# A hybrid encoder layer with product-key experts: both ends reordered, and the routing's table of sums cut from 256 to 144 places

## What is computed

```
h = x + W_out[concat(short gated conv, SSD scan)](RMSNorm(x))
h = h + CrossAttn(RMSNorm(h), 256 memory tokens)
h = h + PEER(RMSNorm(h));   y = RMSNorm(h) * final_norm_w

def block(xb):                                   # PEER, 8 heads, top 16, 128 x 128 experts
    q = (xb @ w_pq).reshape(-1, PEER_HEADS, 2, PEER_DK_HALF)
    sc = einsum('thpd,hpkd->thpk', q, sub_keys)
    v1, i1 = top_k(sc[:, :, 0], 16);  v2, i2 = top_k(sc[:, :, 1], 16)
    comb = (v1[..., :, None] + v2[..., None, :])             # 16 x 16 sums of a head
    cidx = (i1[..., :, None] * N_KEYS + i2[..., None, :])
    top_sc, pos = top_k(comb, 16);  eidx = take_along_axis(cidx, pos)
    gate = softmax(top_sc);  hid = gelu(einsum('td,thkd->thk', xb, u_tab[eidx]))
    return einsum('thk,thkd->td', gate * hid, v_tab[eidx])
```

## Time and profile before

| what | value |
|---|---|
| runs shown (3) | median 1840.97 us, 1833.16 to 1843.06 |
| the profiled execution | 1838.45 us, with a span of 1836.7 us from the first to the last instruction |
| mean granted TensorE clock | 0.963 |
| TensorE matmul (PE) busy | 1689.9 us, 92% |
| DVE busy | 1225.0 us, 67% |
| GpSimd (POOL) busy | 697.7 us, 38% |
| ACT busy | 369.2 us, 20% |
| HBM read and written | 539.46 MB and 21.66 MB |

### The profile page before, as it was taken

One profiled execution on the slowest core, in us unless ns is written; L12 is line 12 of the kernel. 1 busy time (PEld: TensorE's weight loads), 2 busy tenths in 40 slices (PEclk: granted clock), 3 DMA queues, 4 the chain that ended last, 5 costly groups with the idle time before them and its releaser, 6 DMA issues. The chain is left out here.

```text
span 1836.7 us, 19834 instructions
## 1 busy us (share of the span) xinstructions
PE 1689.9 (92%) x7088; PEld 1256.1 (68%) x7088; DVE 1225.0 (67%) x2437; ACT 369.2 (20%) x912; POOL 697.7 (38%) x598
## 2 busy tenths in 40 slices
PE   6998999999777888898896999999999999999996
PEld 5887888877655677787785666666666666666542
DVE  1252111799688768898986999676656666656675
ACT  1031123111330244642660001101000000000101
POOL 0000000234124437731664555555444544534551
PEclk9999999999878999899898999999999999999998
DMA  5532444779336949995999999999999999999995
GB/s 168 180 110 99 153 138 138 240 249 349 101 134 204 379 167 367 338 329 184 361 346 415 409 409 410 409 407 410 406 409 410 397 410 409 396 409 405 377 409 221
DMA packets 238301, 563.10 MB, mean 307 GB/s; under 512 B 17068, under 2 KB 125276, under 8 KB 236156
## 3 DMA queue, kind: packets, MB, share of 16 engines
q0 software_dynamic: 82944, 302.03, 42.7%
q1 hardware_dynamic: 121512, 242.72, 36.1%
q10 hardware_dynamic: 33748, 17.10, 3.1%
HBM read 539.46 MB, written 21.66 MB: 306 GB/s over the span
## 5 line engine op out<-in xcount | busy, mean ns | idle before, releaser
L782 POOL DMA_INDIRECT M<-in_u_tab,IDX x288 | 331.3, 1150 | 736.5 <-DVE PEER L1742 358.0
L789 POOL DMA_INDIRECT M<-in_v_tab,IDX x288 | 362.8, 1260 | 369.2 <-DVE X L1763 299.3
L1093 PE MATMUL PSB<-XN,M 128*128 128x256 f32 x2048 | 469.0, 384 | 12.2 <-ACT M L1303 6.0
L1101 PE MATMUL PSB<-M,HST 128*128 128x512 f32 x1024 | 461.3, 596 | 10.4 <-DVE HST L1819 9.6
L1093 PEld LDWEIGHTS PSB<-XN,M 128*128 128x128 f32 x2048 | 393.5, 193 | 112.8 <-issue 53.2
L1742 DVE CUSTOM_DVE_ANT_0 M<-M,XN 128x1024 f32<-128x1024 f32 x288 | 351.8, 1223 | 146.7 <-DMA M<-in_u_tab,IDX 135.3
L1763 DVE SCALAR_TENSOR_TENSOR X<-M,PEER,X 128x1024 f32<-128x1024 f32 x256 | 328.1, 1282 | 101.4 <-DMA M<-in_v_tab,IDX 88.0
L831 PE MATMUL PSB<-M 128*128 128x256 f32 (+1 forms) x1408 | 333.4, 398 | 10.2 <-DVE M L1399 8.9
L1101 PEld LDWEIGHTS PSB<-M,HST 128*128 128x128 f32 x1024 | 194.8, 191 | 215.1 <-issue 198.5
L831 PEld LDWEIGHTS PSB<-M 128*128 128x128 f32 x1408 | 270.1, 193 | 66.4 <-DVE M L1399 9.8
L838 PE MATMUL PSB<-M 128*128 128x256 f32 (+1 forms) x1056 | 247.7, 395 | 2.5 <-DVE M L1399 1.6
(11 more groups left out here) (214 smaller groups left out, 1072.7 us busy)
## 6 DMA issues: line engine op xcount, KB each, us to landing
M<-in_u_blocks SPq DMA_DIRECT2D x128, 512.0 KB
M<-in_v_tab SPq DMA_DIRECT2D x128, 512.0 KB
M<-in_w_in SPq DMA_DIRECT2D x24, 1024.0 KB
M<-in_w_pq SPq DMA_DIRECT2D x16, 1024.0 KB
gate_spill<-M ACTq DMA_DIRECT2D x16, 1024.0 KB, 14.5
M<-gate_spill SPq DMA_DIRECT2D x16, 1024.0 KB, 11.1
M<-in_w_out SPq DMA_DIRECT2D x8, 1024.0 KB
M<-in_w_mq SPq DMA_DIRECT2D x8, 1024.0 KB
```

The source lines that it names most:

```text
L782: pool.indirect_dma_start(out=UA[:, s % RR, :], out_offset=None, in_=utab, in_offset=bass.IndirectOffsetOnAxis(ap=IDX[:, n:n + 1], axis=0) ...
L789: pool.indirect_dma_start(out=VA[:, s % RR, :], out_offset=None, in_=vtab, in_offset=bass.IndirectOffsetOnAxis(ap=IDX[:, n:n + 1], axis=0) ...
L1093: last = pe.matmul(PSB[:, 4 + b % 2, 0:2 * P], UBLK[:, b % SR, c, :], XN[:, 1:3, c * P:(c + 1) * P], start=(c == 0), stop=(c == DC - 1))
L1101: last = pe.matmul(PSB[:, 2 * t + hf, :], WR[:, b % WRING, t * P:(t + 1) * P], VBLK[:, b % SR, hf * 512:(hf + 1) * 512], start=(b == 0), s ...
```

## The change

1. Start. Tile 1's rows are loaded right after tile 0's. Five of the nine small loads and that of `state_ssd` are issued by SP, between and behind the first big loads. The sum of squares of tile 1 is taken by DVE (`sq`), not ACT, and `const` stands behind tile 0's `norm`.
2. End. `fold` stands ahead of the last `vd`. The first half of that `vd` has a semaphore of its own, for which the first `close` waits. The order of leaving is tile 4, 1, 2, with all three `leave` steps ahead of all three `final` steps.
3. Routing. The table of sums has 8 x 16 sums and 16 more places (8 of them filled with a very small number, 8 with the sums of rows 8 to 15 and column 0). Three instructions of the decoding are added: a `min`, a mask, and for tiles 1 and 2 a copy.
4. The planner's estimate for a piece of `rt` is 1.75 us instead of 1.9.

```diff
@@ dense
-        s += [("const",)]
-        for t in TG[0]:
-            s += [("norm", 0, t), ("turn", 0, t)]
+        s += [("sq", 1), ("norm", 0, 0), ("const",), ("norm", 0, 1), ("turn", 0, 0), ("turn", 0, 1)]
@@ DVE_US
-          "a1": 3.8, "norm": 1.2, "keep": 0.3, "rt": 1.9, "smd": 0.8, ...
+          "a1": 3.8, "norm": 1.2, "keep": 0.3, "rt": 1.75, "smd": 0.8, ...
@@ plan
+        if b == NBLK - 1:
+            out.append(("fold",))
         out.append(("vd", b))
...
-    for t in DENSE:
-        out += [("close", t), ("leave", t), ("final", t)]
-    return out + [("fold",), ("leave", NP), ("final", NP)]
+    out += [("close", t) for t in DENSE] + [("leave", t) for t in CLOSED]
+    return out + [("final", t) for t in CLOSED]
@@ SP
             sp.dma_start(X[:, 0, :], xp[0]).then_inc(x_in[0], 16)
+            sp.dma_start(X[:, 1, :], xp[1]).then_inc(x_in[1], 16)
+            for row in SMALL_ROWS[4:]:
+                load_small(sp, *row)
             load_block(sp, 0)
-            sp.dma_start(X[:, 1, :], xp[1]).then_inc(x_in[1], 16)
             load_block(sp, 1)
+            sp.dma_start(S0[:, :, :], a["state_ssd"]...).then_inc(state_in, 16)
             load_block(sp, 2)
@@ TensorE, vd
+                    if b == NBLK - 1 and t == 0:
+                        last.then_inc(first_closed, 1)
@@ ACT, norm
+                if (ph, t) == (0, 1):
+                    act.wait_ge(sq_done, 1)
+                    col = ROOTS.index(("norm", 0, 1))
+                    act.activation(SS[:, col:col + 1], SS[:, col:col + 1], ACT.Sqrt, bias=EPSC[:, :], scale=1.0 / D).then_inc(root_done, 1)
+                    return
@@ DVE
+            def sq(t):
+                col = ROOTS.index(("norm", 0, t))
+                dve.wait_ge(const_ok, 1)
+                dve.wait_ge(x_in[t], 16)
+                dve.tensor_tensor_reduce(XN[:, t, :], X[:, t, :], X[:, t, :], 1.0, 0.0, ALU.mult, ALU.add, SS[:, col:col + 1]).then_inc(sq_done, 1)
@@ DVE, keys2
-                    also(dve.tensor_tensor(CO, bc(TV[:, 0, :].unsqueeze(2), [P, TOPK, TOPK]), bc(TV[:, 1:2, :], [P, TOPK, TOPK]), ALU.add))
+                    also(dve.tensor_tensor(COF[:, 0:8 * TOPK].rearrange("p (a b) -> p a b", a=8), bc(TV0[:, 0:8].unsqueeze(2), [P, 8, TOPK]),
+                                           bc(TV1.unsqueeze(1), [P, 8, TOPK]), ALU.add))
+                    also(dve.tensor_scalar(COF[:, 8 * TOPK:NCO], TV0[:, 8:24], TV1[:, 0:1], None, ALU.add))
@@ DVE, experts
-                    also(dve.tensor_scalar(CA[:, 0:2, :], CP, 4, 7, ALU.logical_shift_right, ALU.logical_shift_left))
-                    also(dve.tensor_scalar(CA[:, 2:4, :], CP, 15, 7, ALU.bitwise_and, ALU.logical_shift_left))
+                    also(dve.tensor_scalar(CPA[:, 1], CP, 8 * TOPK, None, ALU.min))
...
+                    sync()
+                    also(dve.tensor_scalar(CA, CPA.rearrange("p a z k -> p (a z) k"), 7, None, ALU.logical_shift_left))
...
+                    also(dve.tensor_reduce(EQS, places, AXX, ALU.min))
+                    sync()
+                    also(dve.tensor_scalar(EQS, EQS, NK - 1, None, ALU.bitwise_and))
...
-                        dve.sem_inc(topk_done, 1)
+                        dve.tensor_copy(I12[:, t - 1, :, 2 * TOPK * pair:2 * TOPK * (pair + 1)], EQS).then_inc(topk_done, 1)
@@ DVE, close
-                dve.wait_ge(vd_done, NBLK)
+                if t == DENSE[0]:
+                    dve.wait_ge(first_closed, 1)
+                else:
+                    dve.wait_ge(vd_done, NBLK)
```

More of the change, by code:

```diff
@@ L22 @@
 PH, NK, TOPK = 8, 128, 16
+NCO = 9 * TOPK
 EPS = 1e-6
@@ L145 @@
 DVE_US = {"turn": 1.4, "memn": 2.4, "in": 0.3, "ca": 2.1, "cs": 2.2, "dt": 3.5, "s1": 2.6, "s2": 2.4, "s3": 4.8, "s4": 1.4, "o": 0.45, "mo": 0.45,
-          "a1": 3.8, "norm": 1.2, "keep": 0.3, "rt": 1.9, "smd": 0.8, "tt": 0.6, "oh": 1.25, "d": 1.3, "v": 1.3, "final": 1.3}
+          "a1": 3.8, "norm": 1.2, "keep": 0.3, "rt": 1.75, "smd": 0.8, "tt": 0.6, "oh": 1.25, "d": 1.3, "v": 1.3, "final": 1.3}
 EARLY_STEPS = 5
@@ L517, in build_program @@
         TS2 = take_(2, P)
[L518 to L522, removed]
+        TV0, TV1, TI = take_(3 * 8), take_(TOPK), take_(2, 2, TOPK, u=True)
+        TOPS = [[TV0[:, 0:8], TV0[:, 16:24]], [TV1[:, 0:8], TV1[:, 8:16]]]
+        COF = take_(NCO)
+        CO2 = take_(NCO)
+        CPA = take_(2, 2, TOPK, u=True)
+        take_(1024 - 2 * NCO - 4 * TOPK)
         EQF = cut(PT_, g_[0] - 1024, 1024).bitcast(U32)
-        CP = take_(2, TOPK, u=True)
+        CP = CPA[:, 0]
         CA, KEY = [cut(PT_, 4 * TOPK * k, 4, TOPK).bitcast(U32) for k in range(2)]
-        TAGF = take_(TOPK)
+        TAGF = take_(2, TOPK)
         TAG = TAGF.bitcast(U32)
-        EQS = cut(PT_, 8 * TOPK, 2, 2 * TOPK)
+        EQS = cut(PT_, 8 * TOPK, 2, 2 * TOPK).bitcast(U32)
         SCS = take_(2, 256)
@@ L1658, in keys @@
                     for h in range(2):
-                        also(dve.max(TV[:, h, 0:8], src[:, h, :]))
+                        also(dve.max(TOPS[h][0], src[:, h, :]))
                     sync()
                     for h in range(2):
-                        also(dve.max_index(TI[:, h, z, 0:8], TV[:, h, 0:8], src[:, h, :]))
-                        also(dve.match_replace(TS2[:, h, :], TV[:, h, 0:8], src[:, h, :], NEG))
+                        also(dve.max_index(TI[:, h, z, 0:8], TOPS[h][0], src[:, h, :]))
+                        also(dve.match_replace(TS2[:, h, :], TOPS[h][0], src[:, h, :], NEG))
                 def keys2(z):
@@ L1700, in experts @@
                     places = EQF.rearrange("p (a j k) -> p a j k", a=2, k=TOPK)
-                    if t in DENSE:
-                        also(dve.tensor_reduce(I12[:, t - 1, :, 2 * TOPK * pair:2 * TOPK * (pair + 1)], places, AXX, ALU.min))
-                    else:
-                        also(dve.tensor_reduce(EQS, places, AXX, ALU.min))
+                    also(dve.tensor_reduce(EQS, places, AXX, ALU.min))
+                    sync()
+                    also(dve.tensor_scalar(EQS, EQS, NK - 1, None, ALU.bitwise_and))
                     if (t, pair) == (NP, 0) or pair == PH // 2 - 1:
@@ L1833, in final @@
                 dve.scalar_tensor_tensor(out=x, in0=x, scalar=rs, in1=GAIN[0:n, :], op0=ALU.mult, op1=ALU.mult).then_inc(y_norm, 1)
-            does = {"const": const, "state": state, "norm": norm, "turn": turn, "memn": memn, "in": in_, "keep": keep, "ca": ca, "cs": cs, "dt": dt, "oc": oc,
+            does = {"sq": sq, "const": const, "state": state, "norm": norm, "turn": turn, "memn": memn, "in": in_, "keep": keep, "ca": ca, "cs": cs, "dt": dt, "oc": oc,
                     "kt": kt, "s1": s1, "s2": s2, "s3": s3, "s4": s4, "o": residual("o"), "a1": a1, "mo": residual("mo"),
```

46 lines of the change are left out of this document (26 added, 20 removed).

## The result

| | before | changed |
|---|---|---|
| median of 8 runs | 1840.97 us (1833.16 to 1845.55) | 1827.07 us (1820.83 to 1834.16) |
| ratio, 95% interval | | 0.9937 [0.9918, 0.9957] |
| profiled execution | 1838.45 us, span 1836.7 | 1834.16 us, span 1832.3 |
| mean granted TensorE clock | 0.963 | 0.959 (seven others: 0.961 to 0.967) |
| DVE busy | 1225.0 us | 1213.7 us |

The change takes 13.9 us off the median, 0.6%. Where the two differ, the change is not the cause.

The account below looks back on a forecast made before the run. DVE's in-order queue was taken to hold TensorE up mid-kernel, TensorE's own work to bind behind it, single chains the ends; -5.0 - 1.5 + 4.1 - 5.7 = -8.1 us gave 1830.3 or 1832.9, stated as 1831, range 1821 to 1839.

Parts of the forecast that it names:

- The middle: Between the two ends: moved steps and routing's saving together cost +4.1 us, bounds -9 and +12.
- Start: Start of the kernel: earlier loads let the long matmuls begin at 13.0 us, not 18.03, -5.0 us.
- Clock: First long matmuls: without the long gap between transposes TensorE's clock rises sooner, -1.5 us.
- Routing: Routing on DVE: the smaller table, less its longer decoding, saves 0.75 us of DVE per pair.
- Up to the attention's `norm`: Up to `norm` of group 1's attention: 7.4 us of added steps against 5.6 us of routing saved, +1.0 us.
- Up to `a1`: Up to the scores `a1`: TensorE sets the pace and two `gb` steps are moved ahead, +2.0 us.
- From `a1` to the `norm` of the experts: Group 1, scores to experts' `norm`: DVE ends last, so five added `d`, `v` and `oh` steps cost +5.8 us.
- rival 1: Middle costs nothing or gives: DVE's waits take up the moved steps, middle -6 to +1, about 1825 us; chance 0.22.
- End: End of the kernel: roots and scalings overlap, `fold` goes ahead of the last `vd`, -5.7 us.
- rival 4: End: `fold` waits for DVE's weighted rows and delays the last `vd` by up to 4 us, 1834 us; chance 0.07.
- Rival 2: Middle costs more: group 1's scan is bound by DVE, middle +9 to +14, about 1838 us; chance 0.14.
- rival 3: Scan: moved steps lengthen TensorE's gaps and keep its clock low, +9 us, 1847 us; chance 0.07.

Follow-up runs that it names:

- e0: The changed kernel run and profiled once more, unaltered; median 1824.24 us, ratio to before 0.9915.
- e4: The kernel before with the table of 144 places and its decoding alone, estimate left at 1.9 us; median 1834.83 us, ratio 0.9990.
- e1: The changed kernel with the planner's estimate for a piece of routing back at 1.9 us; median 1819.26 us, ratio to before 0.9907.
- e1b: The changed kernel with the estimate at 1.9 us, run again on another chip; median 1820.39 us, ratio to before 0.9891.
- e1 to e4: Four kernels on one chip: e1, then start, end and table each alone in the kernel before; ratios 0.9907, 0.9973, 0.9979, 0.9990.
- e6: The changed kernel with the planner's estimate for a piece of routing at 2.05 us; median 1815.12 us, ratio to before 0.9852.
- e9: e6 with `fold` behind the last `vd` and tiles leaving in the order 1, 2, 4; median 1812.63 us, ratio to before 0.9859.
- e10: e6 with tile 1's sum of squares on ACT as before, not on DVE; median 1812.86 us, ratio to before 0.9863.
- e6b: e6 run again on another chip, unaltered; median 1816.50 us, ratio to before 0.9878.

## Why the prediction was right or wrong

The forecast (1831 us, faster by 0.4 to 0.5%) was right in its sign and its range; the median lies 4 us below it, at the lower edge of the likeliest case's own range (1827). The two ends carried it. The middle's largest term was wrong, and that the total stayed in the range in spite of it is in part luck. By its steps:

- **Start, -5.0: right.** Measured -5.3 (12.67 against 18.03). The nearest bound, that the small rows land no sooner than 9.88, did not hold: 7.35. The last of these small loads was issued 1.2 us sooner (3.31 against 4.50) and was in 2.5 sooner. Tile 1's rows stayed on SP's queue and moved ahead of the first block: issued 0.5 us sooner (1.26 against 1.74), they were taken up 3.5 sooner (6.05 against 9.54). So what a load gains by its place ahead of the large blocks is more than its issue time. The Trainium skill ("DMA: Bandwidth & Descriptors", section "Issuing engines are not separate DMA queues") says that issuing from several engines saves only issue time. The 3.0 us that the prediction drew from it did not come true, but the rule itself is not refuted: for the small loads no run separates the place from the second queue.
- **Clock, -1.5: the size fits, the reason is not shown.** The first 64 matmuls took 14.08 us in 8 of the 11 profiles with the new start, and 16.1 to 16.5 in the others; with the old start 15.6 to 16.5 in three of three. Over the whole of A the mean is 285.2 us with the new start (11 profiles) and 287.2 with the old (3), with 283.5 to 288.2 and 285.9 to 287.9 inside the two. One kernel lands on either side (14.08 us in the changed kernel's profile, 16.13 in e0), so the new order does not settle it.
- **Routing, -0.75 of DVE per pair: right**, 0.76 measured in e4. That 5.6 us of it are worth as much on TensorE up to the attention's `norm` was right too: B fell by 4.9 in e4, and by 4.7 and 6.6 in e1 and e1b.
- **Up to the attention's `norm`, +1.0: the mechanism right, the term too small.** It measured +3.5 and +1.9. The table gives some 5.4 there, and the order of 1.75 takes 8.3 back (303.6 against 295.25, the means of two profiles each): the 7.4 us of added steps and a little more, and they take out nothing, since the steps of the scan's queue are what TensorE waits for. The waits of TensorE for DVE at the scan's end (L1635) are 17.7 us, 15.4 before.
- **Up to `a1`, +2.0: too large.** In e0 it is -1.3, but 1.7 us of that is the clock: the first 64 matmuls of `q` ran at a granted clock of 0.90 before and 1.00 in e0. These are their lines, before and then e0:

```profile
609.27 17.48 PE L831 MATMUL PSB<-M 128*128 128x288 f32 x64 [1.90 <-DVE M L1399]
```

```profile
608.41 15.79 PE L851 MATMUL PSB<-M 128*128 128x288 f32 x64 [0.51 <-DVE M L1418]
```

  At a like clock it would be about +0.3. The forecast priced the moved `gb` at their length and left out the wait of 3.04 us ahead of the scores, into which they fell. In the changed kernel's own profile the stage is 7.4 us longer, by the late block of `w_mq`, which no term had.
- **From `a1` to the `norm` of the experts, +5.8: this is the step that failed.** It measured -1.4 and -1.7. The steps are there: DVE is busy 87.0 us in the stretch in e0, 80.67 before. But they took the place of DVE's waits for gathered rows. DVE's groups of `v` and `d` in this stretch, before (649 to 755) and then e0 (647 to 751), with the idle time last:

```profile
L1763 DVE SCALAR_TENSOR_TENSOR X<-M,PEER,X 128x1024 f32<-128x1024 f32 x19 | 24.3, 1277 | 2.6 <-DMA M<-in_v_tab,IDX 2.3
L1742 DVE CUSTOM_DVE_ANT_0 M<-M,XN 128x1024 f32<-128x1024 f32 x19 | 23.0, 1215 | 6.0 <-DMA M<-in_u_tab,IDX 6.0
```

```profile
L1795 DVE SCALAR_TENSOR_TENSOR X<-M,PEER,X 128x1024 f32<-128x1024 f32 x21 | 26.9, 1280 | 0.6 <-DMA M<-in_v_tab,IDX 0.5
L1774 DVE CUSTOM_DVE_ANT_0 M<-M,XN 128x1024 f32<-128x1024 f32 x21 | 25.4, 1212 | 2.5 <-DMA M<-in_u_tab,IDX 2.4
```

  Idle time ahead of these two groups fell from 8.6 to 3.1 us, and that of `oh` from 1.5 to nothing: 7.0 us of cover for 6.4 us more work. From the 5.48 us that TensorE waits at the `norm` the forecast concluded that DVE "ends last" and that each step ahead of it is paid. DVE ended last, but behind its own waits for transfers. That is what rival 1 argued. Its own sign of being wrong came too: that wait was to grow to some 9 us and is 5.56 and 4.50. The profiles bear it out on either side. In the six with the order of 1.9 (before, e1 to e4, e1b) DVE's instructions of this stretch take 79.2 or 79.3 us, its waits for gathered rows 6.9 to 9.0, and D 104.5 to 106.4. In the two with that of 1.75 they take 86.3 and 86.5 us, the waits 3.3 and 2.8, and D 104.3 and 104.0.
- **Behind the `norm`, -4.0: right**, -3.3 and -5.6.
- **Tile 2's last pair, -0.7: not visible.** F lies between 149.0 and 154.8 whatever the kernel.
- **End, -5.7: right**, -5.9 (19.9 to 14.04). The order of the roots and scalings came as worked out, and `fold` waited for nothing, so rival 4 has no place.
- **The sum.** The middle was put at +4.1. It is -6.3 in e0 (B to F, 1.7 of it the clock in C) and +6.8 in the changed kernel's profile, 7.1 of it the late block. The medians say what is usual: 13.9 us less 5.3 and 5.9 at the ends leaves -2.7 for middle and clock. Rival 1's middle (-6 to +1) was the better one, and the time fell between its 1825 and the forecast. Rival 2's scan came true in B and was paid back in D and E. The cases' chances add up to 0.47 for faster and 0.46 for within 0.5%, where the prediction has 0.48 and 0.45. Of rival 3 there is little: the granted clock of the scan, 0.89 before, is 0.87 in the changed kernel's profile and 0.89 again in e0.

The new estimate itself is a loss: with the old one the same edits reach 0.9907 and 0.9891, with the new one 0.9937 and 0.9915, some 5 us less (each pair's intervals overlap; B, 8.3 us longer, and the further gain of 2.05 say the same). A lower estimate lets the planner put more gathers into the scan, where each is paid, and takes them from E, where most are hidden. The opposite gains until E is full. In the changed kernel a piece of routing really costs DVE 1.82 us of busy time (217.1 us over 119 pieces) and 1.91 with the short gaps inside it: 1.75 is below that, 1.9 about at it, and 2.05 above. That e6's D (107.8, 107.5) is about 4 us longer than in e9 and e10, which have the same order there, is in part the clock. The first 32 matmuls of the attention's product (L1026) took 6.72 and 6.75 us there and 3.84 in e9 and e10, behind the same wait; the granted clock at that place is 0.54 in e6b and 1.00 in e9. The rest stays open, and so does what makes the block of `w_mq` late: it was late by 4.3 and 3.8 us in two of three profiles with the order of 1.75 ahead of that `norm`, and by 1.7 at most in all others (e9). That the writes of the states, which are issued later there, stand in its way is only argued.

## What to carry to other kernels

A wait of TensorE for DVE does not say that each step more on DVE costs its length: look at what DVE itself waited for in the same stretch, and set those idle microseconds against the added work first. In a planner that fills one engine's queue by estimated costs, an estimate is a lever on where work lands: the true cost was not the best one here, so sweep it, and watch the stage that takes up what is held back. At the ends of a kernel a chain read row by row predicted to within half a microsecond, and there the price of an edit can be measured in a single profile, where the median of runs hardly sees it.
